# A three-block sequence model on one core: scores ahead of transposes, gate preparation beside the sparse attention, ScalarE rounding weights in the search

## What is computed

```python
h = x @ w_in          # dq dk dv | sq sk sv | iq ik iw | fq fk fv ff | gate
lam = exp(sum(lam_q1*lam_k1)) - exp(sum(lam_q2*lam_k2)) + lambda_init
# differential: 4 heads, two maps each
p = softmax(dq1 dk1' / 8) - lam * softmax(dq2 dk2' / 8);   a = p @ dv
# sparse: the index scores pick 256 keys for each query
idx_score = sum_h relu(iq_h ik') * iw_h * 512**-0.5
bo = softmax(sq sk' / 8 over the top 256 of idx_score) @ sv
# forgetting: c = cumsum(log_sigmoid(ff + b_f))
co = softmax(fq fk' / 8 + c_q - c_k) @ fv
x = layer_norm(ALPHA*x + (concat(rms(a)*g, bo, co) * silu(gate)) @ w_out)
```

## Time and profile before

| what | value |
| --- | --- |
| median of three executions | 3628.21 us (3624.89 to 3631.47) |
| the profiled execution's own time | 3621.61 us |
| its span, first to last instruction | 3620.0 us |
| TensorE (PE) busy | 2988.3 us, 83% |
| its weight loads (PEld) | 2344.1 us, 65% |
| VectorE (DVE) / ScalarE (ACT) / GpSimd (POOL) busy | 1693.6 / 954.9 / 724.4 us |
| mean granted TensorE clock | 0.908 of full speed |

### The profile page before, as it was taken

The page is one execution under the profiler, slowest core; times in us unless marked ns, Lnnn a source line. Parts: engine busy times, 40 slices in busy tenths (PEclk is TensorE's granted clock), DMA queues, the critical chain, the costliest instruction groups (busy, mean ns, idle before and its releaser), DMA issues. The chain is left out here.

```text
span 3620.0 us, 38646 instructions
## 1 busy us (share of the span) xinstructions
PE 2988.3 (83%) x14688; PEld 2344.1 (65%) x14688; DVE 1693.6 (47%) x2788; ACT 954.9 (26%) x1832; POOL 724.4 (20%) x475
## 2 busy tenths in 40 slices
PE   6996165697999999969797999767797979997678
PEld 4874054445888888848475887556685657875556
DVE  2002877403323323133789552355435897523555
ACT  2002421202001000020555440344104573412451
POOL 1321001002333333312042203102220323022021
PEclk9998587797999999979898999799898989997989
DMA  2111000201111111031011003003320110021022
GB/s 92 47 35 23 0 1 1 96 6 53 41 58 48 35 65 38 33 126 47 2 64 59 7 1 97 20 1 134 114 72 2 47 64 18 1 76 41 1 100 98
DMA packets 78793, 168.84 MB, mean 47 GB/s; under 512 B 14848, under 2 KB 33680, under 8 KB 78096
## 3 DMA queue, kind: packets, MB, share of 16 engines
q1 hardware_dynamic: 70160, 141.13, 11.7%
q10 hardware_dynamic: 8448, 25.18, 2.5%
HBM read 128.53 MB, written 20.97 MB: 41 GB/s over the span
## 5 line engine op out<-in xcount | busy, mean ns | idle before, releaser
L294 PE MATMUL psum<-H,ffn_W 128*128 128x512 f32 x672 | 262.5, 391 | 13.0 <-POOL ffn_W L1169 11.2
L295 PE MATMUL psum<-H,ffn_W 128*128 128x512 f32 x672 | 262.1, 390 | 0.0
L296 PE MATMUL psum<-H,ffn_W 128*128 128x512 f32 x672 | 261.9, 390 | 0.0
L1167 POOL CAST ffn_W<-ffn_W 128x1024 fp32r<-128x1024 f32 (+1 forms) x84 | 69.3, 825 | 679.3 <-PE psum L296 446.7
L288 PE MATMUL psum<-CONST 128*128 128x512 f32 x116 | 74.0, 795 | 146.0 <-ACT XT_mixer L908 89.2
L1455 ACT ACTIVATE MB<-OM,tk_mid 128x384 bf16<-128x384 f32 (+2 forms) x192 | 157.1, 819 | 111.9 <-DVE tk_mid L1483 111.0
L1486 DVE TENSOR_SCALAR_CACHE_REDUCE MB<-OM,tk_mid 128x512 bf16<-128x512 f32 (+2 forms) x192 | 184.3, 1010 | 2.3
L1393 PE MATMUL psum<-IQ 128*128 128x512 f32 (+3 forms) x384 | 128.8, 502 | 45.8 <-PEq L1884 45.8
L1840 DVE TENSOR_REDUCE df_nmax<-psum 128x1 f32<-128x256 f32 (+7 forms) x128 | 92.9, 753 | 155.9 <-PE psum L1769 155.9
L1169 POOL TENSOR_TENSOR ffn_W<-ffn_W 128x1024 fp32r<-128x1024 f32 (+1 forms) x84 | 161.7, 1926 | 6.7
L1243 DVE TENSOR_SCALAR ffn_Y<-ffn_G,ffn_par 128x1024 f32<-128x1024 f32 x21 | 22.1, 1051 | 297.1 <-ACT ffn_G L1232 297.1
(11 more groups left out here) (413 smaller groups left out, 7594.8 us busy)
## 6 DMA issues: line engine op xcount, KB each, us to landing
OM<-in_w_feat SPq DMA_DIRECT2D x34, 512.0 KB, 4.5
tk_W<-in_w_feat SPq DMA_DIRECT2D x22, 512.0 KB, 3.4
ffn_W<-in_ffn_w_gate SPq DMA_DIRECT2D x21, 512.0 KB, 3.4
ffn_W<-in_ffn_w_val SPq DMA_DIRECT2D x21, 512.0 KB, 3.4
ffn_W<-in_ffn_w_down SPq DMA_DIRECT2D x42, 256.0 KB, 2.7
OM<-MB ACTq DMA_DIRECT2D x64, 128.0 KB, 2.5
OM<-OM ACTq DMA_DIRECT2D x64, 128.0 KB, 2.3
fin_W<-in_w_out SPq DMA_DIRECT2D x4, 2048.0 KB, 10.6
```

The costliest lines, as they stand in the source:

```text
L294: pe.matmul(out, a1, b1, start=start, stop=False)
L295: pe.matmul(out, a1, b2, start=False, stop=False)
L296: return pe.matmul(out, a2, b1, start=False, stop=stop)
L1167: pool.tensor_copy(w1, w).then_inc(rounded, 1)
```

## The change

Five things are changed.

1. `prepare_stage` is gone. A class `Prepare` hands its work in pieces to the sparse stage: SP loads the parameters (`load`), TensorE transposes the logits first (`turn`) and waits after the scores of job 1 until they are read (`wait_read`), ScalarE does Abs first (`bend`) and two Exp and a Ln ahead of job 4 (`log`), VectorE reads the logits first (`begin`) and makes FB and LAM ahead of job 7 (`end`). E and part lie in rows of OS that the sparse stage leaves free. IDX_SCALE is applied in the rotary step of IQ; `identb` and `causalb` are made once, by POOL, in the norm stage before the layers.
2. The sparse stage comes ahead of the forgetting stage. SQ is split in the first projection (`halves`), FQ by POOL in the sparse stage (`split_forget`), with the memset of FB and the cast of `pickb` ahead of it.
3. In the search stage ScalarE casts the weights in POOL's place (`round_on_act`); POOL only subtracts. The schedule of the rounds is 9 (n + 1) // 4. FQ_high is not written there.
4. `low_half` comes one item later in every projection with `halves`.
5. `diff_stage`: `scores(j)` is ahead of the first `turn`, `weigh` ahead of the second. ScalarE takes one group ahead of each exponential; VectorE takes its group of a job's second half after `combine`.

```diff
-                    if halves and n:
+                    if 0 < n <= len(halves):
                         plain, high, _ = halves[n - 1]
                         act.wait_ge(taken_dve, n)
                         act.activation(high, plain, ACT.Copy).then_inc(high_done, 1)
+                def round_on_act(i):
+                    if i >= PARTS:
+                        act.wait_ge(products, i - PARTS + 1)
+                    act.wait_ge(w_in[i % slots], 16 * (i // slots + 1))
+                    width = items[i][1]
+                    act.activation(W1[:, i % PARTS, 0:width], W[:, i % slots, 0:width], ACT.Copy).then_inc(rounded, 1)
+                if beside:
+                    for i in range(PARTS):
+                        round_on_act(i)
                 for n, u in enumerate(by_act):
                     if beside:
-                        beside.count_on_act(act, min(BISECTIONS, 3 * n + 2))
+                        beside.count_on_act(act, (9 * (n + 1)) // 4)
                     act.wait_ge(products, u + 1)
...
+                    if beside and u + PARTS < len(items):
+                        round_on_act(u + PARTS)
                 if beside:
                     beside.count_on_act(act, BISECTIONS)
+                    for i in range(len(units) + PARTS, len(items)):
+                        round_on_act(i)
...
                     w1, w2 = W1[:, i % PARTS, 0:width], W2[:, i % PARTS, 0:width]
-                    pool.wait_ge(w_in[i % slots], 16 * (i // slots + 1))
-                    if i >= PARTS:
-                        pool.wait_ge(products, i - PARTS + 1)
-                    pool.tensor_copy(w1, W[:, i % slots, 0:width]).then_inc(rounded, 1)
+                    if not beside:
+                        pool.wait_ge(w_in[i % slots], 16 * (i // slots + 1))
+                        if i >= PARTS:
+                            pool.wait_ge(products, i - PARTS + 1)
+                    if not beside:
+                        pool.tensor_copy(w1, W[:, i % slots, 0:width]).then_inc(rounded, 1)
                     pool.wait_ge(rounded, i + 1)
                     pool.tensor_tensor(w2, W[:, i % slots, 0:width], w1.bitcast(FP32), ALU.subtract
                                        ).then_inc(split, 1)
-                    if halves and i >= 2:
-                        low_half(pool, i - 2)
+                    if 0 <= i - 3 < len(halves):
+                        low_half(pool, i - 3)
...
-                for n in range(max(0, len(items) - 2), len(halves)):
+                for n in range(max(0, len(items) - 3), len(halves)):
...
+                 v_at=lambda h: 0, prepare=None):
...
+            @block.sync
+            def _(sp):
+                if prepare:
+                    prepare.load(sp)
             @block.tensor
             def _(pe):
+                if prepare:
+                    prepare.turn(pe)
...
+                    if prepare and j == 1:
+                        prepare.wait_read(pe)
...
+                if prepare:
+                    prepare.bend(act)
                 for j in range(J + 2):
+                    if prepare and j == 4:
+                        prepare.log(act)
...
+                if prepare:
+                    prepare.begin(dve)
                 for j in range(J + 2):
+                    if prepare and j == 7:
+                        prepare.end(dve)
...
                 for j in range(J + LAG + 1):
-                    if 0 <= j - LAG < J:
-                        turn(j - LAG, groups_of(j - LAG)[:1])
                     if j < J:
                         scores(j)
                     if 0 <= j - LAG < J:
-                        turn(j - LAG, groups_of(j - LAG)[1:])
+                        turn(j - LAG, groups_of(j - LAG)[:1])
                     if 0 <= j - LAG - 1 < J:
                         weigh(j - LAG - 1)
+                    if 0 <= j - LAG < J:
+                        turn(j - LAG, groups_of(j - LAG)[1:])
...
                 for j in range(J + LAG + 1):
-                    if 0 <= j - LAG < J:
-                        for g in groups_of(j - LAG):
-                            if by_act(g):
-                                take_group(act, g, taken_a, lambda o, i: act.activation(o, i, ACT.Copy))
-                    if j < J:
-                        n = width(j)
-                        if j >= RING:
-                            act.wait_ge(turned, groups_of(j - RING)[-1] + 1)
-                        for m in range(2):
+                    for m in range(2):
+                        if 0 <= j - LAG < J:
+                            for g in groups_of(j - LAG)[m:m + 1]:
+                                if by_act(g):
+                                    take_group(act, g, taken_a, lambda o, i: act.activation(o, i, ACT.Copy))
+                        if j < J:
+                            n = width(j)
+                            if j >= RING and m == 0:
+                                act.wait_ge(turned, groups_of(j - RING)[-1] + 1)
                             act.wait_ge(greatest, 2 * j + m + 1)
...
+                def take_own(j, which):
+                    if 0 <= j < J:
+                        for g in groups_of(j)[which]:
+                            if not by_act(g):
+                                take_group(dve, g, taken_v, lambda o, i: dve.tensor_copy(o, i))
                 for j in range(J + LAG):
                     if j < J:
                         maximum(j, 0)
-                    if 0 <= j - LAG < J:
-                        for g in groups_of(j - LAG):
-                            if not by_act(g):
-                                take_group(dve, g, taken_v, lambda o, i: dve.tensor_copy(o, i))
+                    take_own(j - LAG, slice(0, 1))
                     if j < J:
                         maximum(j, 1)
                     if 0 <= j - 1 < J:
                         combine(j - 1)
+                    take_own(j - LAG, slice(1, 2))
...
+    def wait_read(self, pe):
+        pe.wait_ge(self.bent, 1)
+    def bend(self, act):
+        act.wait_ge(self.read, 1)
+        act.activation(self.E, self.logits.rearrange("p (a n) -> p a n", a=4), ACT.Abs, bias=self.bf).then_inc(self.bent, 1)
+    def log(self, act):
+        act.wait_ge(self.bent, 1)
+        act.activation(self.E, self.E, ACT.Exp, scale=-1.0).then_inc(self.own_a, 1)
+        act.wait_ge(self.ff, 1)
+        act.activation(self.dots, self.dots, ACT.Exp).then_inc(self.exps, 1)
+        act.wait_ge(self.own_a, 1)
+        act.activation(self.E, self.E, ACT.Ln, bias=1.0).then_inc(self.exps, 1)
+    def begin(self, dve):
+        own = self.own = Own(dve, self.own_d)
+        own(dve.memset(self.ones, 1.0))
+        dve.wait_ge(self.params, 96)
+        dve.wait_ge(self.turned, 1)
+        dve.tensor_scalar(self.FF, self.logits, self.bf, 0.0, ALU.add, ALU.min).then_inc(self.read, 1)
+        own.then(dve.tensor_tensor(self.LV[:, 0:2, :], self.LV[:, 0:2, :], self.LV[:, 2:4, :], ALU.mult))
+        dve.tensor_reduce(self.dots, self.LV[:, 0:2, :], AX.X, ALU.add).then_inc(self.ff, 1)
+    def end(self, dve):
+        own, FF, E, part, LAM, dots, init = self.own, self.FF, self.E, self.part, self.LAM, self.dots, self.init
+        by_chunk = lambda ap, a: ap.rearrange("p (a n) -> p a n", a=a)
+        dve.wait_ge(self.exps, 2)
+        dve.wait_ge(self.read, 1)
+        dve.wait_ge(self.zeroed, 1)
+        own.then(dve.tensor_tensor(by_chunk(FF, 4), by_chunk(FF, 4), E, ALU.subtract))
+        own.then(dve.tensor_tensor_scan(FF, self.ones.to_broadcast([4, S]), FF, 0.0, ALU.mult, ALU.subtract))
+        for n in range(3):
+            own.then(dve.tensor_copy(part, by_chunk(FF, 2)))
+            own(dve.tensor_copy(by_chunk(self.FB[32 * n:32 * n + 4, :], 2), part))
+            if n < 2:
+                own.then(dve.tensor_tensor(by_chunk(FF, 2), by_chunk(FF, 2), part, ALU.subtract))
+        own.then(dve.tensor_tensor(LAM[:, 0:1], dots[:, 1:2], dots[:, 0:1], ALU.subtract))
+        own(dve.tensor_tensor(LAM[:, 0:1], LAM[:, 0:1], init[:, 0:1], ALU.subtract))
+        own(dve.tensor_copy(LAM[:, 1:2], init[:, 1:2]))
+        own.wait()
...
+        SQ_high = sbuf(nc, early, "SQ_high", [P, 3, S], FP32R)
...
-        units = [Unit(P, "rope", (dst[m], QK_SCALE if m < 2 else 1.0, (IQ[:, 4, :], IQ[:, 5, :]) if m == 7 else None))
+        units = [Unit(P, "rope", (dst[m], QK_SCALE if m < 2 else IDX_SCALE if 3 <= m < 7 else 1.0, (IQ[:, 4, :], IQ[:, 5, :]) if m == 7 else None))
...
+                      halves=[(SQ[:, m, :], SQ_high[:, m, :], SQ_rest[:, m, :]) for m in range(3)])
-        index_stage(kit, IQ, IW, IS, AM, causal)
+        index_stage(kit, IQ, VS, IS, AM, causal)
...
-            units = [Unit(P, "act", copy_parts(FQ[:, m, :], FQ_high[:, m, :], QK_SCALE if m < 2 else 1.0))
+            units = [Unit(P, "act", copy_into(FQ[:, m, :], scale=QK_SCALE if m < 2 else 1.0))
...
```

(30 more changed lines are left out.)

124 lines of the change are left out of this document (43 added, 81 removed).

## The result

The changed kernel takes 3485.8 us (median of 4 runs, 3481.7 to 3489.8) against 3629.8 for the kernel before (median of 4, the three executions above among them): a ratio of 0.9604, 95% interval 0.9588 to 0.9621. The forecast was 3529 with a range of 3488 to 3574, so the kernel is 43 us faster than forecast and 2 us outside the range. The profiled execution took 3486.4, its span 3484.8, against 3620.0 before.

The account below looks back on a forecast made before the run. Search and sparse stages were taken as near TensorE-bound, the differential stage as waiting, the gate preparation wholly on the path. Terms -48.8 - 2 + 55.6 - 5 - 17.6 - 81 = -98.8 from 3628.2 gave 3529, range 3488 to 3574.

Parts of the forecast that it names:

- Part 1: Gate preparation between first projection and index scores disappears: -24.4 us a layer, -48.8 in all; index stage another -2.
- Part 2: Preparation's work moves into the full sparse stage and stops it at the start, job 4 and job 7: +27.8 a layer.
- cold return: Sparse stage: after a stop TensorE comes back at 0.50 of its clock, 2.8 us each, for two of three stops.
- port rule: Sparse stage: two-input VectorE operations of `end` could each wait for a whole POOL operation; expected not to meet, no cost.
- Part 3: Search stage: ScalarE rounds the weights, bisection ends 7.2 us later, six wide items wait behind it; -5 for two layers.
- Part 4: Last projection: low halves asked for one item later, so four waits for POOL go; 8.8 us a layer, -17.6.
- Part 5: Differential stage: scores ahead of transposes remove TensorE's wait for the combine; stage 128 us, -45 and -36, together -81.
- Half of part 5: Rival, chance 0.20: in the differential stage a wait for the previous job's exponential replaces the combine wait; gain -40, total 3570.
- The reordering does nothing: Rival, chance 0.05: in the differential stage narrow jobs and copies set the pace; no gain there, total 3610.
- The sparse stage absorbing the jobs 4 and 7: Rival, chance 0.17: both insertions use idle time of VectorE and ScalarE; cost only 12 us a layer, total 3497.
- The low clock: Rival, chance 0.03: stops leave TensorE at 1.2 GHz through the sparse and differential stages; +176 us, total 3804.
- Tables: Sparse stage: one table set holding exp and ln would save two 1.28 us loads, 5 us in two layers; chance 0.01.

Follow-up runs that it names:

- early loads: The changed kernel with the six parameter loads issued in the index stage instead of at the start of the sparse stage: 3482.1 us, ratio 0.9598.
- second warm run: The changed kernel with the old differential-stage orders and three idle products of 64 rows by 512 columns in each of 16 narrow jobs: 3621.6 us.
- first warm run: The changed kernel with the old differential-stage orders and four idle 512-column products in each of 16 narrow jobs (up to 4 blocks): 3655.1 us.

## Why the prediction was wrong, point by point

- **Part 1, right.** No stage stands between the projection and the index scores; -24.4 and -23.4.
- **Part 2, right in its sum and in its largest terms.** +27.6 and +22.9 for +27.8. The start came out at 10.4 for 10.6. Job 7 was priced at 9 net of idle time; moving all but the scan away took 9.9 and 7.9 off the stage. The split of POOL was over at 2010.8, before VectorE's `end` at 2023.8, so the port rule of the prediction was not tried there. The 2.8 us for each cold return stayed unproved: idle products at the start of the stage did not shorten the kernel. What the loads cost at the start was taken as lost whole (9.2); with the early loads the clamp waited 4.7 and 3.6 us less and the stage was 5.8 and 2.4 us shorter, so most of that wait was indeed lost.
- **Part 3, right in its mechanism, small.** The bisection ended 6.9 us later after the stage's start (162.8 for 155.9; 7.2 forecast), items 13 to 18 waited behind it, -1.8 and -0.8 for -2.5.
- **Part 4, right.** -9.9 and -8.4; undone, 8.5 and 8.1 come back. One wait for POOL of 2.6 us stayed, where none was forecast. "Nothing" for the halves in the first projection held because the low halves are asked for late there too; otherwise at least 2.0 us a layer of waiting.
- **Part 5, wrong, and here the range failed.** The step is "I take 80% in all: 94 / 0.80 = 118, plus 10 of tail after the last combine = 128". It has two errors of like size. First, the 94 us of TensorE work already hold what it does in that tail: the window behind the last combine, 12.2 us long, had 9.3 of TensorE's busy time, at a clock of 0.86, so 8.0 at full clock, and was counted twice. Counted once, the same 80% gives (94 - 8) / 0.80 + 10 = 117.5, and 118.8 is what the kernel with the scores ahead and nothing else takes. Its fill ahead of the tail, TensorE's busy time at full clock over the length, comes out of its windows as (94.6 - 7.6) / (118.8 - 10.5) = 0.80, so here the guess of 80% itself held; it had no row of its own, and that it did is partly luck. That is 9.2 us a layer. Second, the finer split of the copies and of weigh was given no price at all; it takes the stage from 118.8 to 109.0 and 107.0, 10.8 us a layer, at a fill of 0.87 in layer 0. Both together are the 20 us a layer of the miss. The wide job was close: 5.0 forecast, 4.43 measured, near the 4.5 of TensorE's own work. The bound at 95% is miscounted by 1 us (94 / 0.95 + 10 is 109, so -64 and -55, not -63 and -54); the stage reached it in layer 0 (109.0) and passed it in layer 1 (107.0). Even with this bound the sum would be about 3491, above the 3485.8 measured.
- **The rivals.** Half of part 5: refuted as a time; the wait for the exponential of the job before came, but at 5.6 us a layer, 14.5 with the copies in the old order. The reordering does nothing: refuted. The sparse stage absorbing the jobs 4 and 7: refuted, +27.6 and +22.9. The low clock: refuted for this kernel; in the sparse stage 0.86, in the differential 0.94 and 0.97. Tables: job 4 has two loads of 1.28 us, one on either side of the Ln; the rows are below. The Trainium skill (ScalarE: Activation LUTs, "Table sets: the hidden batching unit") lists a set with both functions; here the trace shows that it is not the one in use.

ScalarE at job 4 of the sparse stage, kernel after:

```profile
2012.97 1.04 ACT L1950 ACTIVATE OM<-OM 4x1024 f32<-4x1024 f32 x1
2013.92 0.19 ACT L1952 ACTIVATE pr_dots<-pr_dots 128x2 f32<-128x2 f32 x1
2014.12 1.28 ACT L1954 ACT_TABLE_LOAD   x1
2015.41 1.05 ACT L1954 ACTIVATE OM<-OM 4x1024 f32<-4x1024 f32 x1
2016.38 0.36 ACT L1693 ACTIVATE sp_PT<-psum 128x256 f32<-128x256 f32 x1
2016.75 1.28 ACT L1709 ACT_TABLE_LOAD   x1
```

And the window of the differential stage's tail, kernel before:

```profile
2457.10:2469.30 12.20, 9.28 (x64) 8.43 (x61) 2.02 (x4) 2.99 (x7) 0.00 (x0) 0.86 0.00 0
```

## What to carry to other kernels

When a stage's length is worked out as work over a fill, ask what of the work the "tail" already contains, and read the tail's own window in the kernel before: its 8 us of work show the double count. When several engines' orders change together, each is a part of its own: one (here TensorE's) can be the gain, the other (the copies) worth nothing alone and 40 us with it. And where a low clock stands beside long waits, take the wait away before warming the engine: in the narrow jobs the clock was 9.6 of 27 us, and most of it came back by itself. An experiment that frees one stage should be read stage by stage: the early loads won 8 us in one and lost them in another, and their total said "nothing".

## What was not expected of the hardware

By its profile, in which the ends of matmuls are modelled, TensorE can be busy without a gap and stay at the lower level of its clock. In the second warm run the narrow jobs were filled with idle products of 64 rows; the granted clock is 0.50 (1.2 of 2.4 GHz) for 36.7 us and rises only then. Windows, narrow part of layer 0:

```profile
2289.30:2326.00 36.70, 36.70 (x138) 23.31 (x137) 14.12 (x49) 13.68 (x53) 0.00 (x0) 0.50 0.00 1
2326.00:2355.30 29.30, 24.29 (x145) 16.50 (x143) 15.41 (x36) 14.22 (x39) 0.00 (x0) 0.89 0.00 1
```

With one fp32 product of 128 rows a job, after a warm start, it stayed at 1.00 while TensorE was busy 42.96 of 53.60 us (above). The Trainium skill (TensorE: Matmul & The Clock Gate, "What's actually happening") says that activity releases the throttle; if busy time is read as activity, the trace of the first of the two disagrees. The start is not what parts them: the first warm run started cold as well (0.56 from 2285 to 2290), had four fp32 products of 128 rows a job, and was at 1.00 over the same stretch of its narrow jobs:

```profile
2294.88:2331.58 36.70, 36.70 (x154) 18.48 (x153) 10.31 (x39) 10.60 (x43) 0.00 (x0) 1.00 0.00 1
```

Rows, data type and the time that the products fill still differ at once, so which of them matters is open.

An idle product of 128 by 512 in fp32 costs 0.86 us at full clock where the projections' products, on rounded operands, follow each other in 0.23; that is why the first warm run decided nothing.
